# A first bias row picked earlier, late modulation steps behind the context's scalings, and the last context product behind the rows' sums

## Chip, cores and metric

The kernel runs on one core of one Trainium2 chip. The metric is the device time of one execution in microseconds, the median of several runs.

## What is computed

Two transformer blocks in sequence, all in float32. x is 256 rows by 1024.

```python
# block 1: attention (two kinds), then a mixture of 32 experts, 4 per row
x = x + gate1 * mixed
h2 = rms_norm(x, norm2_g) * (1 + scale2) + shift2
# per expert: act = (u + 1) * g * sigmoid(1.702 g), g, u clipped; y = act @ w_down + b_down
x = x + gate2 * moe_ffn(h2, ...)

# block 2: two layers on x and on a context xc of 256 rows
for l in range(2):
    mod, modc = silu(c) @ ada_w[l] + ada_b[l], silu(c_ctx) @ ada_w[l] + ada_b[l]
    h  = modulate(rms_norm(x,  mix_pre_g[l]), sh1,  sc1)
    hc = modulate(rms_norm(xc, mix_pre_g[l]), shc1, scc1)
    p = h @ w_in[l]                      # q, k, v, gated MLP, convolution, three gates
    attn = attention(q, [kc; k], [vc; v])  # the rows see the context's keys and values
    y = (ga * attn@w_a + gg * gmlp@w_g + gc * conv@w_c) @ w_out
    x = x + g1 * rms_norm(y)
    x = x + g2 * rms_norm(relu(modulate(rms_norm(x)) @ w1)**2 @ w2)
    if l == 0: the same mixer and MLP for xc, with its own modulation
```

The context's own mixer of layer 0 doesn't depend on x.

## The kernel before

**Weights.** All large weights come from one DRAM array, `stream`, in chunks of 1 MB. SyncE issues them in the order in which they are used into `ring`, a ring of six slots; a slot is filled again when TensorE has counted up `weights_used` for the chunk that was in it. Modulation weights of block 2 are loaded by GpSimd into other buffers.

**Experts.** The stage has 33 experts (e = 0 to 32; the last is a second pass of the expert with most rows). Each works on 64 gathered rows with 12 chunks: four for the gate product, four for the up product (both L862), four for the down product (L970). On TensorE an expert is: wait for the turned inputs (copied by ScalarE, L2495), bias products (L872, they wait for the bias row picked by VectorE: L1893 for expert 0, L1804 for the others), gate product, gather of rows in expert 0 (L879), up product, turning of the next inputs (L899), context work, transposes of the hidden rows (L962), context work, the wait for ScalarE's copy of them (L2514), down product. VectorE clips and multiplies (L1825 to L1845); ScalarE copies the outputs (L2522). The last expert differs: VectorE sums up all experts' rows and gates them (L1789, L1791), then multiplies the last down product by its gate (L1869); two scatters (L904) with a sum each (L1903) end the stage.

**The context's mixer in the experts' gaps.** The mixer of layer 0 for the context is cut into 50 heavy steps (a chunk each, 16 products over 256 columns, L771 or L775) and 41 light ones (transposes, scores, the convolution's mean `mu` and variance `var`). `_place()` (from L86) lays them into the experts: per expert two places for heavy steps, A ahead of the hidden rows' transposes and B behind them, and three for light ones, l1 (after A), l2 (after B) and l3 (after the down product). A heavy step is placed when those it depends on are two moments back and fewer heavy steps are placed than `quota` allows, which grows in a straight line over 65 slots. Experts 33 to 40 are places only; they stand behind the experts. The plan also sets the stream's order: the chunks of A and B come ahead of the expert's ninth chunk. Each engine has its own `context_at(e)` for the same plan. Step `("wo", 3)` is the last: behind it ScalarE sums the squares of both context row tiles (L2288) and VectorE scales and adds them to the context (L1640, L1642; marks `("L0", "x1", 2)` and `("L0", "x1", 3)`). Its buffer `yc` overlaps the first slots of `tmp`.

**Ahead of expert 0** VectorE makes the first selection (`choose(first, 0)`, L1548), four columns of tokens, `busiest()` (the most used expert; among it the reduction L1520 that makes the one-hot columns of experts 0 to 31 from the identity), takes sums of modulations (L1879), normalises the context's rows (L1543), and then copies the first column (L1893).

**Layer 0 of block 2** begins when x is complete: ScalarE's squares (L2288), VectorE's normalisation (L1543), transposes (L573), scalings (`modulated`, L1959), then the products of the convolution's gated pairs (L541 with `features`, eight pairs; ScalarE's sigmoids L2566, VectorE's products L1997). In it VectorE also does the modulation sums of later stages as single steps between its other work: the generators `middle_sums` and `gate_sums` (L1581, L1584 and two foldings). `gate_sums` has 72 steps over four loads; they are taken behind the eight conv products (`take_one("conv", f)`, L2163): 5 each, 18 more behind the fourth and 14 more behind the eighth. Then VectorE scales the context's rows for the MLP (`modulated((L, "h2", 0), ...)`), which TensorE transposes ahead of the output product (`mixed`, L1176); the residual (L1223, L2214, L2217) follows that product's first row tile. GpSimd adds the branches (L2729) and loads modulation weights (L2721) when the sums two loads back are done.

Of the kernel before, what the change touches and what calls it, by code (L numbers as in the profile page):

```python
# [78 lines left out]
def _place():  # L79
# [21 lines left out]
    for pos in range(first, (NBLK + 8) * len(PLACES)):  # L101
        e, w = divmod(pos, len(PLACES))
        w = PLACES[w]
        now = 10 * e + MOMENT[w]
        ready = lambda s: all(done.get(d, now) <= now - (14 if s == ("mu",) else 2) for d in after.get(s, []))
        if w in "AB":
            slots = 2 * (NBLK - START) - 1
            quota = -(-(2 * (e - START) + (w == "B")) * len(HEAVY) // slots)
            if heavy and ready(heavy[0]) and len(HEAVY) - len(heavy) < quota:
                place[e, w] = heavy.pop(0)  # L110
                done[place[e, w]] = now
        else:
            for s in light:
                if ready(s):
                    light.remove(s)
                    place[e, w] = s
                    done[s] = now
                    break
# [109 lines left out]
class Signals:  # L228
# [14 lines left out]
    def mark(self, name, *keys, inc=1):  # L243
        name = self.prefix + name
        self.count[name] = self.count.get(name, 0) + inc
        for key in keys:
            assert (self.prefix, key) not in self.marks, key
            self.marks[self.prefix, key] = (name, self.count[name], self.tag)
        return self.sem(name), inc
# [36 lines left out]
def build(nc, args, known, per):  # L286
    stream, mods_d, mods2_d, cols_d, rows_d, cst_d, x_d, ctx_d, ws_d, wr_d, bd_d, bgu_d, out_d = args
    with ExitStack() as ctx:
# [924 lines left out]
        def _(dve):  # L1213
# [296 lines left out]
            def busiest():  # L1510
# [6 lines left out]
                V.tensor_copy(stat("top"), idx[:, TT, 0:1]).then_inc(*mark("vector_steps"))  # L1517
                TS(stat("over1"), most[:, 0:1], float(2 * CAP), None, ALU.is_gt).then_inc(*mark("vector_steps"))
                TS(stat("over2"), most[:, 1:2], float(CAP), None, ALU.is_gt).then_inc(*mark("vector_steps"))
                V.tensor_reduce(onehot[:, 0:NE], ident.rearrange("p (r e) -> p e r", e=NE), AX, ALU.add).then_inc(*mark("vector_steps"))  # L1520
                dve.wait_ge(*last("vector_steps"))
                TT_(stat("over"), stat("over1"), stat("over2"), ALU.max).then_inc(*mark("vector_steps"))
                TS(onehot[:, NE:NBLK], con("index", 1), stat("top"), None, ALU.is_equal).then_inc(*mark("vector_steps"))
# [22 lines left out]
            def choose(tag, e):  # L1546
                for t in range(TT):
                    i = TS(sel[:, t, :], iot[:, 0:CAP], slot[:, bass.ds(e, 1), t], None, ALU.is_equal)  # L1548
                i.then_inc(*mark("selected", (tag, "sel")))
# [336 lines left out]

            first = ("first", "moe")
            choose(first, 0)
            for n in range(4):
                TS(stat("token", 4)[:, n:n + 1], con("lane", 1), float(P * n), None, ALU.add).then_inc(*mark("vector_steps"))  # L1890
            busiest_then(first)
            iotae_b = con("iotae", NE).unsqueeze(1).unsqueeze(1).to_broadcast([P, TT, TOPK, NE])
            V.tensor_copy(pickrow, onehot[:, 0:1].to_broadcast([P, CAP])).then_inc(*mark("row_picked", (first, "row")))  # L1893
            places()
            for e in range(NBLK):
                prev = ("moe", e - 1) if e else first
# [1 line left out]
            for t in range(TT):  # L1898
# [3 lines left out]
                    xs = x[:, t, 512 * h:512 * h + 512]  # L1902
                    i = TT_(xs, xs, ps[:, 6 + h, :], ALU.add)  # L1903
                i.then_inc(*mark("sums_updated", (tag, "y+", t)))
            for e in range(NBLK, NBLK + 8):
                for place in PLACES:
                    context_at(e)(place)
            dve.wait_ge(*at("flag"))
            over = nc.vector.value_load(flag[0:1, 0:1], min_val=0, max_val=1)
            with nc.vector.If(over > 0):  # L1910
# [54 lines left out]
            for l in range(LAYERS):  # L1965
# [5 lines left out]
                if l == 0:  # L1971
                    coefficients(0, (0,))
                    modulated((L, "h"), [(0, TT, 0)], 0)
                V.memset(glp[:, :, :, 0:PADT], 0.0).then_inc(*mark("vector_steps"))
                dve.wait_ge(*last("vector_steps"))
                V.memset(glp[:, :, :, SEQ + PADT:SEGW], 0.0).then_inc(*mark("vector_steps"))
# [223 lines left out]
                for f in range(KD):  # L2200
                    if f < 4:
                        dve.wait_ge(*at((L, "added", "attn", f + 4)))
                    take_one("conv", f)
                    for _ in range(5 + (18 if f == 3 else 14 if f == KD - 1 else 0)):
                        next(gates, 0)
                for _ in gates:
                    pass

                def residual(which, t, ready):

# [7 lines left out]
                    dve.wait_ge(*last("x_updated"))  # L2218
                if l == 0:
                    modulated((L, "h2", 0), [(TT, 2 * TT, 1)], 24)  # L2220
                for t in range(nt):
                    residual(0, t, "x1")
                    normalise(L, "n2", t, "xn2")
                    if l:
                        modulated((L, "h2", t), [(t, t + 1, 0)], 24)
# [47 lines left out]
        def _(act):  # L2273
# [257 lines left out]
            context_squares()  # L2531
            for e in range(NBLK):
                expert(("moe", e), e >= STORED, e < NE, (e,), context_at(e))
            for e in range(NBLK, NBLK + 8):
                for place in PLACES:
                    context_at(e)(place)
            act.wait_ge(*at("flag"))
            over = nc.scalar.value_load(flag[0:1, 0:1], min_val=0, max_val=1)
            with nc.scalar.If(over > 0):
# [10 lines left out]
            for l in range(LAYERS):  # L2550
# [7 lines left out]
                if l == 0:  # L2558
                    for t in range(TT):
                        sumsq((("L0", "n1"), t), rowsx[t:t + 1], junkb, [("x2", t)])  # L2560
                for k in range(KD):
                    kb = ((L, "cg"), 2 * k + 1)
                    act.wait_ge(*at(("full", kb)))
                    if k >= 4:
                        act.wait_ge(*at(("drained", ((L, "cg"), 2 * k - 8))))
                    A(tmp[:, k % 4, 0:N], ps[:, B(kb), 0:N], ACT.Sigmoid).then_inc(*mark("gates_ready", ("drained", kb)))  # L2566
# [394 lines left out]
```

## Time and profile before

| | us |
|---|---|
| median of 3 runs | 3087.0 (3080.79 to 3092.16) |
| the profiled execution | 3087.64 |
| its span | 3085.8 |
| TensorE busy | 2912.4 |
| VectorE busy | 1269.2 |
| ScalarE busy | 459.8 |
| GpSimd busy | 80.9 |

The span runs from the first to the last instruction. A busy TensorE is not one at its peak: matmuls are pipelined and their ends are modelled. The mean granted TensorE clock was 0.984 of full speed. The transfers moved 762.08 MB, 247 GB/s over the span; the experts' stage, from about 280 us to 1535, runs near 400 GB/s.

In the rows further down a window gives its length, the busy time (and count of instructions) of PE (TensorE's matmuls), PEld (its weight loads), DVE (VectorE), ACT (ScalarE) and POOL (GpSimd), the granted TensorE clock, the mean busy share of the DMA engines and what they moved. A row of the timeline gives start, duration, engine, line, operation, output and input and the count of instructions merged, and in brackets the idle time of that engine just before and who ended it.

### The profile page before, as it was taken

The numbers are of one execution on the slowest core, as the hardware profiler recorded it, in microseconds if no ns is written. First come the engines' busy times: TensorE is split into PE (matmuls) and PEld (weight loads), VectorE is DVE, ScalarE is ACT, GpSimd is POOL, SyncE is SP. The second block draws the span as 40 slices with busy tenths as digits, with TensorE's granted clock in tenths as the row PEclk, the third lists the DMA queues.
The fourth block names the chain that finished last, engine by engine and source line by source line (L and its number), as shares of the span: only waits on it lengthen the run. The fifth ranks groups of instructions, "written<-read, shape, count | busy, mean of one in ns | idle before, by whom it ended". The sixth has DMA issues, their size and how long they took to land.

```text
span 3085.8 us, 31210 instructions
## 1 busy us (share of the span) xinstructions
PE 2912.4 (94%) x12164; PEld 1724.0 (56%) x12164; DVE 1269.2 (41%) x3060; ACT 459.8 (15%) x921; POOL 80.9 (3%) x107
## 2 busy tenths in 40 slices
PE   5998999999999999998799999999999999999998
PEld 3464455555545444444387588544444677587764
DVE  6754112444441121111368856383582268731101
ACT  1212001222211110000202131110000111311100
POOL 0000000000000000001000001000000000000000
PEclk9988999999999999999999999999999999999999
DMA  8556999999999989999753324342441344124342
GB/s 330 223 225 268 405 387 394 389 399 395 394 399 387 398 359 402 392 406 401 321 196 144 137 76 177 115 176 97 163 164 55 109 149 149 57 109 164 111 163 95
DMA packets 110497, 762.08 MB, mean 247 GB/s; under 512 B 12976, under 2 KB 13360, under 8 KB 21776
## 3 DMA queue, kind: packets, MB, share of 16 engines
q1 hardware_dynamic: 95040, 699.44, 57.3%
q0 software_dynamic: 8240, 45.88, 4.0%
q10 hardware_dynamic: 7072, 14.76, 1.3%
q8 instruction: 99, 1.62, 0.2%
q14 instruction: 46, 0.38, 0.0%
HBM read 749.81 MB, written 10.22 MB: 246 GB/s over the span
## 4 chain that ended last, share of the span: by engine, by line
PE 82%; DMA 10%; DVE 6%; ACT 1%; issue 1%; DVEq 0%; SPq 0%; ACTq 0%
PE ps L541 26%; PE ps L553 17%; DMA ring<-stream 9%; PE ps L862 8%; PE ps L775 8%; PE ps L970 7%; PE ps L771 3%; PE ps L1176 2%; PE ps L1164 1%; PE ps L573 1%; PE ps L602 1%; PE ps L872 1%; PE ps L615 1%; DMA area<-modulation 1%; DVE area L1242 1%
## 5 line engine op out<-in xcount | busy, mean ns | idle before, releaser
L541 PE MATMUL ps<-area,ring 128*128 128x256 f32 (+1 forms) x3328 | 820.8, 409 | 0.3
L541 PEld LDWEIGHTS ps<-area,ring 128*128 128x128 f32 x3328 | 633.3, 191 | 183.8 <-issue 108.1
L553 PE MATMUL ps<-ring,area 128*128 128x512 f32 x1216 | 528.4, 596 | 4.0 <-DVE area L2263 4.0
L862 PE MATMUL ps<-ring,area 128*64 128x512 f32 x2112 | 479.7, 599 | 40.6 <-DMA ring<-stream 40.0
L553 PEld LDWEIGHTS ps<-ring,area 128*128 128x128 f32 x1216 | 232.0, 191 | 290.9 <-issue 285.3
L862 PEld LDWEIGHTS ps<-ring,area 128*64 128x64 f32 x2112 | 142.3, 137 | 376.1 <-issue 268.9
L775 PE MATMUL ps<-area,ring 128*128 128x256 f32 x1152 | 255.5, 380 | 0.0
L970 PE MATMUL ps<-ring,area 128*64 128x512 f32 x1056 | 237.1, 602 | 9.2 <-ACT area L2514 9.2
L775 PEld LDWEIGHTS ps<-area,ring 128*128 128x128 f32 x1152 | 216.0, 190 | 28.5
L2015 DVE SCALAR_TENSOR_TENSOR area<-area,cols 128x256 f32<-128x256 f32 x480 | 201.7, 483 | 1.1
L1584 DVE SCALAR_TENSOR_TENSOR cst<-area,cond,cst 128x256 f32<-128x256 f32 x448 | 183.0, 482 | 0.0
L970 PEld LDWEIGHTS ps<-ring,area 128*64 128x64 f32 x1056 | 73.6, 138 | 152.7 <-issue 141.7
L1840 DVE TENSOR_SCALAR area<-ps 128x512 f32<-128x512 f32 x33 | 22.8, 691 | 239.3 <-PE ps L862 239.3
L573 PE MATMUL ps<-cst,area 128*128 128x128 f32 x416 | 70.6, 311 | 40.7 <-DVE area L1959 17.5
L1825 DVE TENSOR_SCALAR area<-ps 128x512 f32<-128x512 f32 x33 | 22.8, 692 | 208.8 <-PE ps L862 208.8
L771 PE MATMUL ps<-ring,area 128*128 128x256 f32 x448 | 101.3, 385 | 3.6 <-ACT area L2506 2.3
L2248 DVE TENSOR_TENSOR area<-area 128x512 f32<-128x512 f32 (+1 forms) x64 | 34.7, 556 | 163.4 <-ACT area L2681 162.8
L1617 DVE SCALAR_TENSOR_TENSOR area<-area,cols 128x256 f32<-128x256 f32 x240 | 97.8, 477 | 0.1
L573 PEld LDWEIGHTS ps<-cst,area 128*128 128x128 f32 x416 | 55.0, 160 | 71.1 <-issue 41.8
L771 PEld LDWEIGHTS ps<-ring,area 128*128 128x128 f32 x448 | 85.2, 193 | 15.8 <-ACT area L2506 2.5
L1804 DVE COPY area<-area 128x64 f32<-128x64 f32 x32 | 6.2, 192 | 186.2 <-PE ps L872 186.2
L2681 ACT ACTIVATE area<-ps 128x512 f32<-128x512 f32 (+1 forms) x64 | 31.4, 491 | 294.3 <-PE ps L541 262.1
(342 smaller groups left out, 2043.6 us busy)
## 6 DMA issues: line engine op xcount, KB each, us to landing
ring<-stream SPq DMA_DIRECT2D x642, 1024.0 KB, 8.8
area<-shared_modulation POOLq DMA_DIRECT2D x32, 1024.0 KB, 5.1
area<-modulation SPq DMA_DIRECT2D x16, 1536.0 KB, 6.6
expert_rows<-area ACTq DMA_DIRECT2D x62, 128.0 KB, 7.2
x<-x_tiles ACTq DMA_DIRECT2D x1, 1024.0 KB, 12.9
area<-ctx_tiles ACTq DMA_DIRECT2D x1, 1024.0 KB, 4.9
input_rows<-area ACTq DMA_DIRECT2D x4, 256.0 KB, 2.0
out<-x SPq DMA_DIRECT2D x2, 512.0 KB, 2.6
```

What stands on the lines that cost most here:

```text
L541: i = mm(ps[:, b, 0:n], w[:, k % 4, j * P:(j + 1) * P], rhs(k), start=(k == 0), stop=(k == 4 * kgs - 1))
L553: i = mm(ps[:, b, :], lhs(k, t), w[:, k % 4, :], start=(k == 0), stop=(k == 4 * kgs - 1))
L573: i = nc.tensor.transpose(ps[:, b, j * P:(j + 1) * P], src(j), ident)
L771: ins = mm(ps[:, b, j * SEQ:(j + 1) * SEQ], src[:, k, j * P:(j + 1) * P], w[:, k, :], start=(k == 0), stop=(k == KD - 1))
L775: ins = mm(ps[:, b, j * SEQ:(j + 1) * SEQ], w[:, k, j * P:(j + 1) * P], src, start=(k == 0), stop=(k == KD - 1))
L862: i = mm(ps[half(h), bank, :], xT[:, k % 4, half(k // 4)], w[:, 2 * (k % 2) + h, :], start=False, stop=(k == KD - 1))
L970: i = mm(ps[half(h), APART if apart else DOWN, :], actT[:, k % 4, half(k // 4)], w[:, 2 * (k % 2) + h, :], start=(k == 0), stop=(k == KD - 1))
L1176: i = mm(ps[:, b, :], merged[:, k, t * P:(t + 1) * P], chunk(c)[:, k % 4, :], start=(k == 0), stop=(k == KD - 1))
L1584: i = STT(acc, w[:, k], c, acc, ALU.mult, ALU.add)
L1617: i = STT(cvc(k), src, w(k, tap), cvc(k), ALU.mult, ALU.add)
L2015: i = STT(dst, src, w(k, tap), dst, ALU.mult, ALU.add)
L2248: TT_(hid[:, j, 0:NF], tmp[:, j % 8, 0:NF], tmp[:, j % 8, 0:NF], ALU.mult).then_inc(*mark("hidden_ready", (L, "hid", hf, j)))
```

## The change

In `_place()` the quota grows over two slots more. The reduction leaves `busiest()`; it and the copy of the first bias row follow the first selection. The loops over the places of experts 33 to 40 move on VectorE behind layer 0's first scalings, and on ScalarE behind the squares of x, where a wait for the context's last addition is added ahead of the first sigmoid. TensorE's loop stays where it was, behind the last scatter. The last 19 of the `gate_sums` steps move from behind the eighth conv product to behind the scaling of the context's rows. The loader and the plan of the stream follow the placement.

```diff
@@ _place
-            quota = -(-(2 * (e - START) + (w == "B")) * len(HEAVY) // slots)
+            quota = -(-(2 * (e - START) + (w == "B")) * len(HEAVY) // (slots + 2))
@@ vector: busiest
-                V.tensor_reduce(onehot[:, 0:NE], ident.rearrange("p (r e) -> p e r", e=NE), AX, ALU.add).then_inc(*mark("vector_steps"))
@@ vector: ahead of the experts
             choose(first, 0)
+            V.tensor_reduce(onehot[:, 0:NE], ident.rearrange("p (r e) -> p e r", e=NE), AX, ALU.add).then_inc(*mark("vector_steps"))
+            dve.wait_ge(*last("vector_steps"))
+            V.tensor_copy(pickrow, onehot[:, 0:1].to_broadcast([P, CAP])).then_inc(*mark("row_picked", (first, "row")))
             for n in range(4):
                 TS(stat("token", 4)[:, n:n + 1], con("lane", 1), float(P * n), None, ALU.add).then_inc(*mark("vector_steps"))
             busiest_then(first)
             iotae_b = con("iotae", NE).unsqueeze(1).unsqueeze(1).to_broadcast([P, TT, TOPK, NE])
-            V.tensor_copy(pickrow, onehot[:, 0:1].to_broadcast([P, CAP])).then_inc(*mark("row_picked", (first, "row")))
             places()
@@ vector: behind the rows' last sums
-            for e in range(NBLK, NBLK + 8):
-                for place in PLACES:
-                    context_at(e)(place)
             dve.wait_ge(*at("flag"))
@@ vector: layer 0
                     coefficients(0, (0,))
                     modulated((L, "h"), [(0, TT, 0)], 0)
+                    for e in range(NBLK, NBLK + 8):
+                        for place in PLACES:
+                            context_at(e)(place)
@@ vector: conv branch
-                    for _ in range(5 + (18 if f == 3 else 14 if f == KD - 1 else 0)):
+                    for _ in range(0 if f == KD - 1 else 23 if f == 3 else 5):
                         next(gates, 0)
-                for _ in gates:
-                    pass
...
                 if l == 0:
                     modulated((L, "h2", 0), [(TT, 2 * TT, 1)], 24)
+                    for _ in gates:
+                        pass
@@ scalar: behind the experts
-            for e in range(NBLK, NBLK + 8):
-                for place in PLACES:
-                    context_at(e)(place)
             act.wait_ge(*at("flag"))
@@ scalar: layer 0
                     for t in range(TT):
                         sumsq((("L0", "n1"), t), rowsx[t:t + 1], junkb, [("x2", t)])
+                    for e in range(NBLK, NBLK + 8):
+                        for place in PLACES:
+                            context_at(e)(place)
+                    act.wait_ge(*at(("L0", "x1", 2 * TT - 1)))
```

## Rows read from the trace of the kernel before

**Rows 1.** Page, the chain that ended last, by engine.

```profile
PE 82%; DMA 10%; DVE 6%; ACT 1%; issue 1%; DVEq 0%; SPq 0%; ACTq 0%
```

**Rows 2.** Windows by expert, from one down product (L970) to the next.

```profile
333.22:373.78 40.56, 38.08 (x186) 19.89 (x188) 4.78 (x11) 2.81 (x5) 0.95 (x1) 1.00 1.00 413
...
608.48:642.78 34.30, 32.62 (x166) 15.61 (x168) 14.64 (x37) 7.56 (x12) 0.95 (x1) 1.00 0.98 399
...
832.22:860.07 27.85, 26.53 (x146) 11.08 (x148) 16.71 (x41) 2.42 (x4) 0.95 (x1) 1.00 1.00 400
...
860.07:903.33 43.26, 40.51 (x198) 21.83 (x200) 20.50 (x50) 6.69 (x12) 0.94 (x1) 1.00 0.96 396
...
1054.95:1101.21 46.26, 44.10 (x217) 26.16 (x216) 16.43 (x31) 10.85 (x16) 0.94 (x1) 1.00 0.85 335
...
1357.70:1397.49 39.79, 38.01 (x186) 20.06 (x188) 3.78 (x9) 2.91 (x5) 0.95 (x1) 1.00 0.98 408
...
1397.49:1430.31 32.82, 30.81 (x152) 13.95 (x153) 4.83 (x10) 2.91 (x5) 0.94 (x1) 1.00 0.98 389
```

**Rows 3.** Timeline around expert 0, several engines.

```profile
268.89 0.41 DVE L1548 TENSOR_SCALAR area<-cst,area 128x64 f32<-128x64 f32 x2
...
270.24 0.37 DVE L1520 TENSOR_REDUCE area<-cst 128x32 f32<-128x128 f32 x1
...
273.80 0.60 ACT L2495 ACTIVATE area<-ps 128x512 f32<-128x512 f32 x1 [1.77 <-PE ps L899]
...
279.61 0.19 DVE L1893 COPY area<-area 128x64 f32<-128x64 f32 x1
...
279.94 1.98 PE L872 MATMUL ps<-area 32*64 32x512 f32 x8 [6.18 <-DVE area L1893]
...
281.85 8.82 PE L862 MATMUL ps<-ring,area 128*64 128x512 f32 x32
...
292.22 7.03 PE L862 MATMUL ps<-ring,area 128*64 128x512 f32 x32
...
310.86 1.09 PE L872 MATMUL ps<-area 32*64 32x512 f32 x8
```

**Rows 4.** Window of two microseconds ahead of expert 0.

```profile
276.00:278.00 2.00, 0.00 (x0) 0.00 (x0) 0.74 (x2) 1.99 (x3) 0.00 (x0) 0.50 0.00 0
```

**Rows 5.** Timeline of the last two experts and layer 0's begin.

```profile
1467.34 7.17 PE L771 MATMUL ps<-ring,area 128*128 128x256 f32 x32
...
1506.84 8.86 PE L771 MATMUL ps<-ring,area 128*128 128x256 f32 x32 [2.26 <-ACT area L2506]
...
1516.37 1.06 ACT L2288 ACTIVATE area<-area 128x1024 f32<-128x1024 f32 x1
...
1520.64 0.59 ACT L2514 ACTIVATE area<-ps 128x512 f32<-128x512 f32 x1
...
1521.29 8.62 PE L970 MATMUL ps<-ring,area 128*64 128x512 f32 x32 [4.93 <-ACT area L2514]
...
1530.53 0.69 DVE L1869 TENSOR_TENSOR area<-ps,area 128x512 f32<-128x512 f32 x1
...
1533.89 1.13 PE L904 MATMUL ps<-area 64*128 64x512 f32 x4 [1.48 <-DVE x L1903]
...
1542.33 3.65 PE L573 MATMUL ps<-cst,area 128*128 128x128 f32 x16 [7.31 <-DVE area L1543]
...
1554.14 0.38 ACT L2566 ACTIVATE area<-ps 128x256 f32<-128x256 f32 x1 [11.64 <-PE ps L541]
```

**Rows 6.** Timeline in layer 0 between the conv branch and the residual.

```profile
1924.50 0.42 DVE L2163 TENSOR_TENSOR area<-ps,area 128x256 f32<-128x256 f32 x1
...
1934.42 2.04 PE L573 MATMUL ps<-cst,area 128*128 128x128 f32 x8 [9.14 <-DVE area L1959]
...
1936.26 28.22 PE L1176 MATMUL ps<-ring,area 128*128 128x512 f32 x64
...
1952.59 0.15 DVE L1223 TENSOR_SCALAR stats<-stats 128x1 f32<-128x1 f32 x1 [15.06 <-ACT area L2288]
```

## The prediction

> **What bounds the kernel now.** I read the chain of waits first [rows 1]: matmuls hold 82% of it, transfers 10%, VectorE 6%. So time is saved only where TensorE stands idle, runs at the lower of its clock levels, or takes turns with the weight stream. The windows by expert [rows 2] show the last: each window runs from one expert's down product to the next one's. With two heavy context steps it takes some 40 us, and TensorE is busy for 38 of them. With one it takes 33 to 34; TensorE is busy for 31 to 33 of them and the transfer share is 0.98. So TensorE sets an expert with two steps, the stream one with fewer. The timeline ahead of the first expert [rows 3] shows TensorE idle for 6.18 us until VectorE has copied the first bias row. The one around the last expert [rows 5] shows it waiting 4.93 us for ScalarE's copy and 7.31 us for the rows' scaling. The one in layer 0's mixer [rows 6] shows 9.14 us of idle time ahead of the transposes of the second row set.
>
> **First bias row, and the reduction that feeds it.** The copy (0.19 us) starts at 279.61 because the normalisation of the context's rows stands ahead of it [rows 3]. It needs only a reduction of a constant (0.37 us). Both now follow the first selection, which ends at 269.30; they are through by about 269.9. TensorE's next condition is ScalarE's copy of the turned inputs, which ends at 274.40 [rows 3]. So the biases start at about 274.45, 5.5 us earlier. Behind the old place of the copy stand VectorE's row numbers and the selection for the next gather. They keep their times, some 2 us after 279.61, and TensorE wants the selection only after the gate product, at 274.45 + 1.09 + 7.03 = 282.6: just in time. The idle time also costs clock: the granted clock is 0.50, the 1.2 GHz level, at 276 to 278 [rows 4]. The biases take 1.98 us there and 1.09 at the upper level, the first gate product 8.82 and 7.03 [rows 3]: 2.7 us more. The stream cannot hold this back: it moves 0 GB/s at 276 to 278 [rows 4], since the ring's six chunks are full and the first is freed by the gate product; it restarts earlier by the same 8.2 us. I take **-8.2**; if the clock falls all the same, -5.5; nothing if another wait stood at 279.9, for which no row speaks.
>
> **Planner's quota.** I worked out the placement from the rule as the code has it. Before: experts 0 and 1 none, then two steps in 20 experts up to 31, one in 9, none in expert 15, one in 32. After: two in 18, one in 12, expert 15 gets one, one in 32, and the last step (wo, 3) in slot 33, behind the experts. The 17 undisturbed windows with two steps (first and last of them shown) average 39.71 us, the 9 with one (first and last shown) 33.86. The window without a step takes 27.85, but its successor 43.26, so with the carry it is worth 31.4 [rows 2]. The change up to expert 31: 2 x 39.71 + 31.4 against 3 x 33.86, that is -9.2 us. Of this 5.85 is the step that leaves, the rest comes from evening out. Bounds: if bytes alone counted, one chunk of 1.05 MB at 400 GB/s [rows 2], -2.6; on the other side -9.2.
>
> Two places within it differ. The context's variance step moves from ahead of ScalarE's copy for the down product to behind it, with a heavy step of TensorE over the mean step's squares. The window that holds it now has 46.26 - 44.10 = 2.2 us of idle TensorE [rows 2]; I take **-2.2**, bounds 0 and -3.8 (with the slower down product behind such a wait, 8.62 against 7.03 [rows 5]). In expert 9 the step (qkv, 5) now stands alone in the first slot, with its square, root and VectorE's sum ahead of that same copy and no second heavy step over it. The nearest row is the 4.93 us wait of the last expert [rows 5]; most of it falls into time in which such an expert waits for the stream, so +1.0, bounds 0 and +4.9. Together **-10.4**.
>
> A page of the Trainium skill speaks against this term. "DMA: Bandwidth & Descriptors", Where 436 GB/s comes from, says that the HBM side binds transfers into SBUF at about 358 GB/s per core. The windows but the disturbed one show 389 to 413 GB/s [rows 2], so the trace doesn't agree. By the rule the 13 chunks of a window with one step (13.6 MB) would need 38 us, every expert would be set by bytes, and the term would be one chunk, an estimated -2.9; the sum would be that of the first rival.
>
> **The last expert and what follows.** Now (wo, 3) runs in the last expert's first slot: 8.86 us of TensorE, then on ScalarE a copy, two passes of squares (from 1516.37) and a root with an answer from VectorE, and only then the copy for the down product at 1520.64, so the down product starts at 1521.29 and takes 8.62 at a fallen clock. VectorE does four context operations and four of the totals, and its product of the last rows starts at 1530.53 [rows 5]. After: (wo, 2) stands in the second slot, behind the transposes of the hidden rows and beside ScalarE's copy. 1506.84 + about 1.0 for two groups of transposes + 8.86 + 7.03 without the idle time = 1523.7. VectorE's totals need only the gate row of 1506.8 and end by 1512. The product of the rows comes 6.5 us earlier, and the two scatters with it.
>
> (wo, 3) then falls into TensorE's 7.31 us between the last scatter and the transposes [rows 5]. At the upper level it takes 7.17, and the first transpose, which takes its bank, also waits for ScalarE's 0.6 us copy: +0.5. In return TensorE keeps its clock: the first sigmoid now stands at 1554.14, 8.2 us after the transposes, where a pair of features is 16 products like a context step's, 7.17: -1.0. Queued behind the moved VectorE part (about 5 us of four additions and scalings) are the padding and the first gated product; ScalarE's added wait stands ahead of its first sigmoid. Both are due about 8 us after the transposes begin to be scaled, as now, and TensorE has four banks, nearly 14 us, before it needs one back. I cost this at nothing; without that cover it would be up to 11 us. Together **-7.0**; bounds -2 and -8.5.
>
> **Late modulation steps.** The 19 steps behind the last conv product ran from 1924.92 (end of that product [rows 6]) until the scaling on which the transposes wait for 9.14 us. Moved behind the scaling they free it at 1924.9; the transposes resume about 0.6 us later, at 1925.5 instead of 1934.42. **-8.9**. The output product then starts at about 1927.3 instead of 1936.26. The steps, 9 us on VectorE, now run to about 1937.7; what follows them is the residual, due 16.3 us after the output product's start (1952.59 - 1936.26), so at 1943.6: 6 us to spare. GpSimd's next modulation load follows them by some 4 us, and nobody reads it before the next stage. Bounds -6 and -9.7 (the clock no longer falls in the gap).
>
> **The sum.** -8.2 - 10.4 - 7.0 - 8.9 = -34.5 us. From the profiled execution's 3087.64 us (span 3085.8 and 1.8 around it) this gives **3053 us**; the median of the runs is 3087.0, so it needs no shift.
>
> **Rivals.**
> *The stream sets the experts.* Bytes don't change; if TensorE's share of an expert is only borrowed from the ring's store, the quota gives one chunk's time. For it: a transfer share of 0.96 and more in all windows shown but the disturbed one. Against it: 5.85 us per step instead of 2.6. 3087.6 - 8.2 - 2.6 - 7.0 - 8.9 = 3061.
> *The last context step becomes the wait.* ScalarE stands at the added wait while TensorE fills its banks: 11 us back (about 4 of squares and root, 5 of VectorE, the rest between them). For it: the root needs VectorE, which is at the scalings. Against: four banks. 3064.
> *Slower: context steps in the second slot hold ScalarE and VectorE when the next expert needs them.* Twelve steps move from first to second slot in their expert. If each cost what the variance step does, 2.2 of idle time and 1.6 of clock, that is 46 us, and the sum 3099. It decides from the tenth such stall. Against it: the copy that the down product needs now stands ahead of them, and the down product (7 us) and the next gate product (7 us) cover them.
> *The gain is given back.* The earlier start is lost before the end, because something not in these rows has its own time: 3083. Nothing in the layers is timed otherwise than by TensorE.
>
> **Chances.** Forecast 0.65, stream 0.20, last step 0.08, slower 0.04, given back 0.03. Range: from all terms at their better ends with the runs' scatter, 3043, to the first two rivals with a term short, 3069. A measurement of this kernel tells about 0.5%, 15 us, from no change. All but the last two cases lie beyond it on the fast side: faster 0.92, same 0.05, slower 0.03.
>
> **What would show it.** The copy of the first bias row at about 270, the first gate product in 7.0 us and a clock of 1.00 ahead of it. Windows of 34 and 39.7 us, 12 and 18 of them. No idle time of TensorE ahead of the last down product, (wo, 3) behind the last scatter. The output product directly behind the second row set's transposes. It would be wrong if windows with one step took 36 us or more, if the first sigmoid came more than 9 us after the transposes, or if the residual waited for the modulation steps.

## The result and the profile after

| | before | after |
|---|---|---|
| median | 3088.58 us (4 runs) | 3054.99 us (4 runs) |
| range | 3080.79 to 3092.16 | 3053.54 to 3056.72 |
| span of the profiled execution | 3085.8 | 3052.6 |
| TensorE busy | 2912.4 | 2903.9 |
| mean granted clock | 0.984 | 0.990 |

The ratio is 0.9898, with a 95% interval of 0.9886 to 0.9910: 31.5 us faster by the ratio (the two medians differ by 33.6, the profiled spans by 33.2). In a later series the same kernel had 0.9896 (0.9878 to 0.9915). Bytes are unchanged (762.08 MB), and so is the chain by engine but for a point [rows 1]:

```profile
PE 83%; DMA 9%; DVE 5%; ACT 1%; issue 1%; DVEq 0%; SPq 0%; ACTq 0%
```

**Ahead of expert 0.** The timeline of the changed kernel, several engines, against [rows 3]:

```profile
269.21 0.42 DVE L1547 TENSOR_SCALAR area<-cst,area 128x64 f32<-128x64 f32 x2
...
269.94 0.20 DVE L1890 COPY area<-area 128x64 f32<-128x64 f32 x1
...
274.12 0.60 ACT L2496 ACTIVATE area<-ps 128x512 f32<-128x512 f32 x1 [1.77 <-PE ps L899]
...
274.82 1.40 PE L872 MATMUL ps<-area 32*64 32x512 f32 x8 [0.73 <-issue]
...
276.14 8.42 PE L862 MATMUL ps<-ring,area 128*64 128x512 f32 x32
```

and the window against [rows 4]:

```profile
276.00:278.00 2.00, 2.00 (x10) 0.63 (x8) 0.42 (x2) 1.97 (x3) 0.00 (x0) 0.50 0.00 0
```

The copy is at 269.94 and the biases follow ScalarE's copy of the turned inputs, as forecast. But the clock is at its lower level, 1.2 GHz, in this window although TensorE is busy through all of it, and the gate product takes 8.42 us, not 7.03. Expert 0's down product starts at 297.22 (before 303.33): 28.0 us after the start of the selection at 269.21, against 34.4 before. That is 6.4 us.

**The windows by expert**, from down product to down product, against [rows 2]:

```profile
565.24:597.99 32.75, 32.18 (x166) 15.75 (x168) 15.95 (x38) 7.78 (x15) 0.94 (x1) 1.00 0.99 406
597.99:635.23 37.24, 32.75 (x167) 15.59 (x168) 15.24 (x37) 8.72 (x14) 0.95 (x1) 1.00 1.01 419
...
821.69:856.51 34.82, 33.46 (x179) 17.15 (x180) 17.47 (x42) 7.71 (x14) 0.94 (x1) 1.00 1.01 410
856.51:896.81 40.30, 39.74 (x202) 22.30 (x204) 22.23 (x54) 6.30 (x11) 0.94 (x1) 1.00 0.96 390
...
1042.67:1090.00 47.33, 44.84 (x218) 26.07 (x220) 7.33 (x13) 7.22 (x11) 0.94 (x1) 1.00 0.89 362
1090.00:1122.41 32.41, 30.52 (x154) 14.07 (x156) 13.37 (x26) 6.53 (x10) 0.94 (x1) 1.00 0.93 375
```

They are experts 8, 9, 15, 16, 21 and 22. From expert 0's down product to expert 31's it is 1164.24 us, before 1171.19: -6.95, where -10.4 was forecast. The one-step windows but expert 9's average 33.5 us, the two-step ones but experts 21 and 31 39.9. Expert 9's takes 37.24.

**The last expert and layer 0's begin**, against [rows 5]:

```profile
1495.19 8.18 PE L771 MATMUL ps<-ring,area 128*128 128x256 f32 x32
...
1503.31 7.09 PE L970 MATMUL ps<-ring,area 128*64 128x512 f32 x32
...
1510.51 0.69 DVE L1868 TENSOR_TENSOR area<-ps,area 128x512 f32<-128x512 f32 x1 [11.67 <-PE ps L970]
...
1514.92 7.17 PE L771 MATMUL ps<-ring,area 128*128 128x256 f32 x32
...
1522.79 2.94 PE L573 MATMUL ps<-cst,area 128*128 128x128 f32 x16 [0.69 <-ACT area L2433]
...
1534.01 0.38 ACT L2568 ACTIVATE area<-ps 128x256 f32<-128x256 f32 x1
1534.53 0.42 DVE L1998 TENSOR_TENSOR area<-ps,area 128x256 f32<-128x256 f32 x1 [1.25 <-ACT area L2568]
```

(wo, 2) runs straight into the down product, (wo, 3) lies behind the last scatter, and the transposes wait 0.69 us instead of 7.31. From the first bound, expert 31's down product, to the last product (L1868) it is 49.1 us, before 56.1: -7.0. From there to the transposes 12.28 against 11.80: +0.5. From the transposes to the second sigmoid 16.79 against 18.71: -1.9.

**The second row set's transposes**, against [rows 6]:

```profile
1903.45 1.80 PE L573 MATMUL ps<-cst,area 128*128 128x128 f32 x8 [0.15 <-DVE area L1957]
...
1920.90 0.15 DVE L1223 TENSOR_SCALAR stats<-stats 128x1 f32<-128x1 f32 x1 [5.48 <-ACT area L2289]
```

The output product starts at 1905.09, 2.82 us after the first set's transposes (1902.27), before 12.02: -9.2. It and its surroundings last 28.62 us against 29.24: -0.6. The residual finds VectorE idle for 5.48 us, so the moved steps are hidden.

The sum: +0.3 (the selection came later) - 6.4 - 6.95 - 7.0 + 0.5 - 1.9 - 9.2 - 0.6 = -31.3 of the -33.2 between the two spans. 0.5 more lies in layer 0 between, and 1.4 in the 1100 us behind, spread over many stages; I did not follow it.

### The profile page after: what moved, and what is told of

The parts are those of the page before. It is cut to its first block, busy times and chain, and to the rows that moved or that the text cites. A ratio compares the mean times of both kernels' runs of the same rounds, so it can differ in the third digit from the quotient of the medians.

```text
span 3052.6 us, 31208 instructions
## 1 busy us (share of the span) xinstructions
PE 2903.9 (95%) x12164; PEld 1719.6 (56%) x12164; DVE 1269.7 (42%) x3060; ACT 457.1 (15%) x919; POOL 80.7 (3%) x107
## 2 busy tenths in 40 slices
DMA packets 110497, 762.08 MB, mean 250 GB/s; under 512 B 12976, under 2 KB 13360, under 8 KB 21776
## 4 chain that ended last, share of the span: by engine, by line
PE 83%; DMA 9%; DVE 5%; ACT 1%; issue 1%; DVEq 0%; SPq 0%; ACTq 0%
PE ps L541 27%; PE ps L553 17%; DMA ring<-stream 9%; PE ps L862 8%; PE ps L775 8%; PE ps L970 7%; PE ps L771 3%; PE ps L1176 2%; PE ps L1164 1%; PE ps L573 1%; PE ps L602 1%; PE ps L872 1%; PE ps L615 1%; DMA area<-modulation 1%; DVE area L1242 1%
## 5 line engine op out<-in xcount | busy, mean ns | idle before, releaser
L862 PE MATMUL ps<-ring,area 128*64 128x512 f32 x2112 | 478.7, 599 | 38.1 <-DMA ring<-stream 37.5
L970 PE MATMUL ps<-ring,area 128*64 128x512 f32 x1056 | 235.4, 598 | 0.0
L970 PEld LDWEIGHTS ps<-ring,area 128*64 128x64 f32 x1056 | 73.2, 137 | 142.4 <-issue 142.0
L573 PEld LDWEIGHTS ps<-cst,area 128*128 128x128 f32 x416 | 53.3, 156 | 56.8 <-issue 34.4
```

Source lines behind the costliest of these rows:

```text
L573: i = nc.tensor.transpose(ps[:, b, j * P:(j + 1) * P], src(j), ident)
L862: i = mm(ps[half(h), bank, :], xT[:, k % 4, half(k // 4)], w[:, 2 * (k % 2) + h, :], start=False, stop=(k == KD - 1))
L970: i = mm(ps[half(h), APART if apart else DOWN, :], actT[:, k % 4, half(k // 4)], w[:, 2 * (k % 2) + h, :], start=(k == 0), stop=(k == KD - 1))
```

## Experiments

Each is given by its edit against the kernel before or the changed one. Kernels of a series share their runs of the kernel before; its medians were 3087.0, 3085.6, 3087.9 and 3091.4 us, so the ratios are compared, not the times. Of e8_clock there is one run, of e10_half there are two.

### One part alone

**e1_row**, on the kernel before:

```diff
             choose(first, 0)
+            V.tensor_reduce(onehot[:, 0:NE], ident...)
+            V.tensor_copy(pickrow, onehot[:, 0:1]...)      # both deleted at their old places
```

> Only the first bias row and its reduction are moved. Theory, after the trace of the changed kernel (biases 5.1 us earlier, gate product still 8.42 us): the term stands alone and is worth 6 us, ratio 0.9980. Rival 1, the prediction's own term: 8.2 us, ratio 0.9973. Rival 2, the start is lost again within the experts because the stream has its own time: under 2 us, ratio 0.9994 or more.

Measured: 0.9980 (0.9971 to 0.9989), 6.2 us. In its profiled execution the clock did not fall; TensorE's timeline:

```profile
277.51 1.09 PE L872 MATMUL ps<-area 32*64 32x512 f32 x8 [0.73 <-issue]
278.53 7.09 PE L862 MATMUL ps<-ring,area 128*64 128x512 f32 x32
```

The down product comes 26.3 us after the selection, against 33.7 to 34.4 in the four profiles with the copy at its old place: there the forecast's term of 8.2 is nearly reached. In six profiles of kernels that share the changed kernel's order here (it, its repetition, and e5, e6, e7 and e9 below) the gate product took 8.36 to 8.57 us and the distance was 27.9 to 28.0; in a seventh, of e10 below, 9.26 and 29.4.

**e2_late**, on the kernel before:

```diff
-                    for _ in range(5 + (18 if f == 3 else 14 if f == KD - 1 else 0)):
+                    for _ in range(0 if f == KD - 1 else 23 if f == 3 else 5):
...
                     modulated((L, "h2", 0), [(TT, 2 * TT, 1)], 24)
+                    for _ in gates:
+                        pass
```

> Only the late modulation steps are moved. Theory: the idle time ahead of the second row set's transposes goes from 9.14 us to under 0.3, the output product takes 27.5 us instead of 28.2 and nothing behind it is late: 9.8 us, ratio 0.9968. The prediction had 8.9, ratio 0.9971. Rival: the steps delay the residual or the next load and part comes back: 6 us or less, ratio 0.9981 or more.

Measured: 0.9973 (0.9963 to 0.9983), 8.3 us. It agrees with 8.9 as with 9.8, but the interval reaches down to 5.2 us, so the runs alone don't exclude the rival's 6. The trace does, as far as one goes:

```profile
1926.68 27.63 PE L1176 MATMUL ps<-ring,area 128*128 128x512 f32 x64
...
1942.49 0.15 DVE L1223 TENSOR_SCALAR stats<-stats 128x1 f32<-128x1 f32 x1 [5.47 <-ACT area L2288]
```

The output product starts 2.82 us after the first set's transposes, the MLP's first product follows 28.62 us later, both as in the changed kernel, and the residual finds VectorE idle.

**e3_plan**, the kernel before with the quota and the moved loops:

```diff
-            quota = -(-(...) * len(HEAVY) // slots)
+            quota = -(-(...) * len(HEAVY) // (slots + 2))     # and both loops moved, as in the change
```

> Quota and moved loops, without the other two parts. Theory: 7.0 us up to the last expert's down product, 7.0 in the last expert, 1.4 behind it: 15.4 us and, with what the two traces leave unassigned, up to 17; ratio 0.9950. The prediction had 17.4 us (0.9944). Rival, the stream sets the experts: 2.6 + 7.0 = 9.6 us, ratio 0.9969. If the parts only add up together (a faster part uncovers another), this one and the two single parts sum to less than the 33.6 us of the whole.

Measured: 0.9960 (0.9946 to 0.9974), 12.3 us. The rival's 0.9969 lies in the interval too. The three sum to 26.9 us with some 6 us of uncertainty; 31.5 for the whole is inside it. The parts add up as far as can be told.

**e4_quota**, the quota alone, both loops at their old place.

> The quota alone: the loops over the places behind the experts stay in VectorE's and ScalarE's old place, ahead of the rows' squares. The last context product is then on TensorE behind the last scatter, and ScalarE's copy, squares and root and VectorE's additions stand ahead of the squares of x. Theory: 11 us of the gain come back (7.2 of product, 4 of ScalarE and VectorE), so 4 us faster than before, ratio 0.9986, and TensorE idle for some 18 us ahead of the transposes. Rival, the loops' place is worth nothing because the product lies in a gap anyway: as with the loops moved, 0.995.

Measured: 1.0009 (1.0000 to 1.0018): not 4 us faster but 3 slower. The timeline at layer 0's begin, three engines:

```profile
1524.50 7.17 PE L771 MATMUL ps<-ring,area 128*128 128x256 f32 x32
...
1540.46 1.22 DVE L1642 TENSOR_TENSOR area<-area 128x1024 f32<-128x1024 f32 x1
...
1542.17 1.06 ACT L2288 ACTIVATE area<-x 128x1024 f32<-128x1024 f32 x1 [4.42 <-DVE stats L1933]
...
1547.74 3.65 PE L573 MATMUL ps<-cst,area 128*128 128x128 f32 x16 [16.06 <-DVE area L1543]
```

From the last product to the transposes it is 27.65 us instead of 12.28, so the place of the loops is worth 15.4 us, more than quota and last expert together. I had expected 11, the product and ScalarE's part, and left out VectorE's additions, which end only at 1541.7 with the squares of x behind them. The quota by itself gains nothing. The moved loops by themselves hold no step, since with the old quota (wo, 3) lies in the last expert; only together do the two gain.

**e5_noquota**, the changed kernel with the old quota (`// slots`).

> The changed kernel with the old quota: 50 steps in the experts, nothing in the moved loops. Theory, the quota is worth what the trace of the changed kernel shows (7.0 us up to the last expert's down product, 7.0 in the last expert, 0.5 lost and 1.9 won behind it): 15.4 us slower than the changed kernel, ratio to before 0.9948. If the run with quota and loops alone tells the size (12.3 us), ratio 0.9938. Rival, the stream sets the experts: 9 us slower than the changed kernel, ratio 0.9927. The idle time ahead of the first transposes should be 7.3 us again and the last down product should wait some 5 us for ScalarE.

Measured: 0.9944 (0.9930 to 0.9958), 14 us slower than the changed kernel, between the two sizes that the theory gave; the stream's 0.9927 is just outside. Both waits came back:

```profile
1514.39 10.09 PE L970 MATMUL ps<-ring,area 128*64 128x512 f32 x32 [4.93 <-ACT area L2515]
...
1536.39 3.65 PE L573 MATMUL ps<-cst,area 128*128 128x128 f32 x16 [7.30 <-DVE area L1542]
```

### How much cover there is

**e6_cover**, on the changed kernel:

```diff
                         r = rstd_of(("C", "y"), TT, D)
+                        for _ in range(8):
+                            TT_(yc[:, 0, :], yc[:, 0, :], yc[:, 0, :], ALU.max)...
```

> The changed kernel, with eight more VectorE operations of about 1.23 us on the first context row tile between the root and the scalings of the last context step (they leave its values as they are): the added wait ends some 9.9 us later. Theory, four banks cover: the first gated product stood at 1534.5 and TensorE needs the first bank back two pairs (13.8 us) after its first product at 1525.6, so 4.9 us are spare and 5 of the 9.9 us show: idle TensorE of 5 us in the features' products, ratio 0.9914. Rival 1, no cover, the wait was already on the path: 9.9 us, ratio 0.993. Rival 2, nothing of it is on the path: 0.9898.

Measured: 0.9925 (0.9912 to 0.9939), 8 us slower. TensorE, timeline:

```profile
1526.25 13.98 PE L541 MATMUL ps<-area,ring 128*128 128x256 f32 x64
...
1544.56 30.70 PE L541 MATMUL ps<-area,ring 128*128 128x256 f32 x129 [4.33 <-DVE area L2001]
```

TensorE ran for 13.98 us, two pairs, into its four banks and then waited 4.33 us. That is the forecast's cover with its length. But the idle time had a second price: the granted clock was 0.63 from 1542 to 1546, the end of the wait included, and 0.52 from 1546 to 1550, and from the first product of the features to the transposes behind the conv branch it was 384.2 us against 376.7 in the changed kernel, 7.5 for an idle time of 4.3. The interval includes rival 1's 0.993; the trace rules it out.

**e7_spare**, on the changed kernel:

```diff
                     for _ in gates:
                         pass
+                    for _ in range(10):
+                        TT_(x[:, 0, :], x[:, 0, :], x[:, 0, :], ALU.max)...
```

> The changed kernel, with ten more VectorE operations of about 1.23 us on the first row tile (values as they are) behind the moved modulation steps: 12.3 us more ahead of the residual. Theory: the residual had 5.5 us to spare (its idle time in the changed kernel), so it comes 6.8 us late; what follows it on TensorE is the transposes of the rows for the MLP behind the output product, so up to 6.8 us show if nothing else lies over them, ratio up to 0.992. Rival 1, the spare is larger because TensorE is still in the second row tile of the output product: 0, ratio 0.9898. Rival 2, the steps already held the residual: all 12.3 us, 0.9938.

Measured: 0.9912 (0.9897 to 0.9928), 4 us slower. The residual came 7.2 us late by the trace, as expected. Of these, TensorE's wait ahead of the MLP's first product (L1164) shows 2.95 us instead of 1.00, and the product took 15.59 us instead of 14.05 at a granted clock of 0.66 from 1939 to 1943: 3.5 us. So beyond VectorE's 5.5 us there are about 5 more in which only VectorE is late, under the second row tile of the output product.

### What sets an expert

**e10_half**, on the changed kernel:

```diff
                 for j in range(2):
-                    for k in range(KD):
+                    for k in range(0, KD, 2):          # in context_heavy of TensorE; stop= moved to match
```

> The changed kernel with half of the products left out of every heavy context step (16 of 32, so 3.55 us of 7.1 us of TensorE; the context's values are therefore not computed); every byte is still loaded. Theory: an expert with two steps is set by TensorE (39.9 us), one with one step by the stream (33.5 us for 13 chunks, 2.58 us each). With half the products two steps take 14 chunks, 36.1 us, and one step still 33.5: 18 x 3.8 = 68 us less, the transfer share near 1.00 in all windows; about 2985 us, ratio 0.967. Rival 1, the stream sets every window already: under 10 us less, ratio 0.987. Rival 2, TensorE sets every window: 30 x 1.6 x 3.55 = 170 us less, ratio 0.935.

Measured: 0.9680 (0.9649 to 0.9710), 0.967 expected. Windows of experts 7 (two steps), 8 (one), 11 (two) and 12 (one):

```profile
510.85:546.92 36.07, 32.12 (x157) 14.08 (x156) 14.48 (x36) 6.87 (x11) 0.94 (x1) 1.00 1.01 420
546.92:582.05 35.13, 30.29 (x150) 12.19 (x149) 16.94 (x42) 7.53 (x15) 0.95 (x1) 1.00 1.01 421
...
652.21:688.25 36.04, 33.62 (x165) 15.72 (x164) 17.07 (x40) 9.11 (x16) 0.95 (x1) 1.00 1.01 420
688.25:721.96 33.71, 30.32 (x149) 12.68 (x148) 15.76 (x39) 7.99 (x14) 0.94 (x1) 1.00 1.01 422
```

Look at the last two columns: with half of the context steps' products gone the stream runs at 420 GB/s in these windows (415 to 423 in 29 of the 32 windows from expert 1 on; less in 21, 22 and 32), and 55 chunks (experts 5 to 8) take 144.1 us, 2.62 each. At that pace an expert with two steps costs some 36 us and one with one step 34. So in the changed kernel a two-step expert (39.9) is set by TensorE and a one-step expert (33.5) by the stream, and a step more or less is worth about 6 us, not one chunk.

**e9_turn**, on the changed kernel, for the wait in expert 9:

```diff
 PLACE = _place()
+PLACE[9, "l2"], PLACE[9, "l3"] = PLACE[9, "l3"], PLACE[9, "l2"]
```

> The changed kernel with two light steps of expert 9 in each other's place: (score, 1) ahead of the down product, (turn, 5) behind it. In the changed kernel (turn, 5) waits 2.66 us for VectorE ahead of the down product, since (qkv, 5) stands alone in the first slot and no heavy step covers its norm. Theory: the window of expert 9 goes from 37.2 to 34.6 us and most of it stays: 2 to 2.7 us, ratio 0.989. Rival, the stream takes it: the window's transfer share is 1.01, so the product waits for the same chunk two experts on and nothing is won, 0.9898.

TensorE's waits in the changed kernel from 290 to 1540 (engine, line, for whom, us, times, longest):

```profile
PE ps L862 <- DMA ring<-stream: 37.5, 65, 1.6
PE ps L962 <- DVE area L1844: 12.6, 10, 1.4
PE ps L797 <- DVE area L1678: 2.7, 1, 2.7
```

and in the kernel before:

```profile
PE ps L862 <- DMA ring<-stream: 40.0, 68, 1.7
PE ps L970 <- ACT area L2514: 9.2, 5, 4.9
PE ps L962 <- DVE area L1845: 7.8, 7, 1.4
```

Measured: 0.9885 (0.9870 to 0.9901), not told apart from the changed kernel. The wait of 2.66 us is replaced by one of 1.18 for ScalarE, the windows of experts 9 and 10 are

```profile
597.25:633.55 36.30, 33.17 (x167) 15.89 (x168) 14.27 (x34) 9.41 (x15) 0.95 (x1) 1.00 1.01 420
633.55:673.68 40.13, 39.36 (x198) 21.68 (x200) 17.94 (x44) 8.13 (x15) 0.95 (x1) 1.00 0.93 376
```

0.9 shorter and 0.6 longer than in the changed kernel's profile (37.24 and 39.52): 0.3 us for both, which looks like the rival. But the sum of these two windows varies by itself: in seven profiles with the changed plan (the changed kernel, e3, e4, e6, e7, e8 and e12) it is 76.8 to 79.9 us with a mean of 78.2, and the changed kernel's own is the least of them. Here it is 76.4, and 76.1 in e11_more below. So the theory's 2 us and the rival's nothing both stay possible, in the trace as in the runs.

**e11_more**, on the changed kernel, three edits:

```diff
+PLACE[9, "B"] = PLACE.pop((9, "A"))
+PLACE[9, "l2"], PLACE[9, "l3"] = PLACE[9, "l3"], PLACE[9, "l2"]
+PLACE[22, "l2"] = PLACE.pop((21, "l2"))
...
-            for n in range(PAIRG + 2, PAIRG + PAIRL):
-                fold_pair(n)
+            fold_pair(PAIRG + 2)
             turn_rows(first)
+            fold_pair(PAIRG + 3)
```

> The changed kernel with three more edits of the order: (qkv, 5) alone in the second slot of expert 9 with (turn, 5) behind the down product; the variance step one expert later, in expert 22, which has one heavy step and waits for the stream; expert 0's inputs turned between the two foldings ahead of it. Theory: 3 us (expert 9's window from 37.2 to some 34), 1.5 us (expert 21's 47.3 us lose 3.6 of TensorE work, expert 22's 32.4 take it partly into waits for the stream), 0.6 us: 5 us faster than the changed kernel, ratio to before 0.988. Rival, stalls taken away only let the stream fall behind, and the waits for it take all of it back: ratio as of the changed kernel.

**e12_again**, the changed kernel unaltered, in the same series.

> The changed kernel once more, on the same chip as the one above: 0.9898 as the first time if the other kernels' differences of 3 to 6 us are to be read at their face value; its interval says how far they can be.

Measured: 0.9879 (0.9860 to 0.9897) for e11_more and 0.9896 (0.9878 to 0.9915) for e12_again. That e11_more beats the changed kernel isn't shown. The windows of its experts 9, 21 and 22:

```profile
594.24:629.90 35.66, 33.20 (x166) 15.75 (x168) 14.55 (x36) 7.66 (x13) 0.94 (x1) 1.00 1.01 420
...
1042.81:1086.00 43.19, 41.16 (x203) 23.09 (x204) 7.76 (x15) 5.34 (x9) 0.94 (x1) 1.00 0.91 377
1086.00:1123.01 37.01, 34.41 (x170) 16.96 (x172) 4.41 (x8) 4.30 (x6) 0.94 (x1) 1.00 0.98 396
```

Expert 21 gave 4.1 us and expert 22 took 4.6: the moved step's 3.6 us of TensorE work only changed places. TensorE's wait for VectorE in (turn, 5) is gone from the stage, and so is the one for ScalarE that e9_turn had in its place. The waits of the gate and up products for the stream were 43.6 us, against 37.5 in the changed kernel and 34.3 to 39.7 in the seven profiles with its plan. From expert 0's to expert 31's down product it took 1170.6 us, no less than in those (1161.6 to 1169.9). The third edit shows ahead of expert 0: the clock stayed, and its down product came 25.8 us after the selection instead of 28.0.

```profile
273.30 7.09 PE L865 MATMUL ps<-ring,area 128*64 128x512 f32 x32
```

### The clock ahead of expert 0

**e8_clock**, on the changed kernel:

```diff
+            for d in range(8):
+                mm(ps[half(d % 2), GATE, :], ident[:, 0:64], xn1[:, d % 2, 0:512], start=True, stop=True)
             turn_rows(first)
+            for d in range(4):
+                mm(...)                                     # the same
```

> The changed kernel with twelve extra products of 128x512 into a bank that is overwritten later: eight ahead of the turning of expert 0's inputs (1.8 us), four between it and the biases. Theory, the clock falls because TensorE has idle time and only narrow products (128x2, 128x128) there: with wide products it stays at 1.00, the biases take 1.09 us and the gate product 7.03 instead of 1.40 and 8.42; the down product of expert 0 comes 1.8 - 1.7 = 0.1 us later than in the changed kernel, counted from the first selection (27.9 us there). Rival, the fall has nothing to do with what TensorE does in these few us: the gate product still takes 8.4 us and the down product comes 29.7 us after the selection.

TensorE's timeline:

```profile
277.10 3.65 PE L992 MATMUL ps<-area,cst 128*64 128x512 f32 x16
...
281.27 1.94 PE L995 MATMUL ps<-area,cst 128*64 128x512 f32 x8
283.14 1.09 PE L872 MATMUL ps<-area 32*64 32x512 f32 x8
284.15 7.09 PE L862 MATMUL ps<-ring,area 128*64 128x512 f32 x32
```

The clock stayed, as the theory has it. The size was off: a product counts as two instructions of 0.23 us each, so the twelve take 5.6 us, and the down product came 31.0 us after the selection, 3.1 later than in the changed kernel. One profile doesn't prove the cause, since e1_row kept its clock without them, and e11_more kept it with a folding moved behind the turning and no more idle time than 0.35 us ahead of the biases. As a gain the twelve products are useless: they cost more than the clock gives back.

## Why the prediction was right, step by step

3053 was forecast, 3055 came. Part of that is luck: by the two traces two terms were too large by 5 us, two too small by 2, and 2 lie where nothing was forecast.

| step | forecast | the two traces | by runs |
|---|---|---|---|
| first bias row | -8.2 | -6.4 | -6.2 (-9.0 to -3.4) |
| quota, up to expert 31 | -10.4 | -7.0 | |
| last expert, (wo, 3), clock | -7.0 | -8.4 | |
| these two | -17.4 | -15.4 | -12.3 (-16.7 to -8.0) alone; -14 by taking the quota back |
| late modulation steps | -8.9 | -9.8 | -8.3 (-11.4 to -5.2) |

**First bias row.** The 5.5 us of idle time were right (the biases came 5.4 us earlier, counted from the selection). The 2.7 us of clock were the mis-sized term: 1.0 came back, since the clock fell with TensorE idle for only 0.73 us, behind two foldings of narrow products and four transposes. The fallback named there, -5.5, was nearer (0.9 us off, and the value taken 1.8). Whether it falls isn't settled by the instructions alone: e1_row had the same ones here and kept 1.00. The Trainium skill's "TensorE: Matmul & The Clock Gate", What's actually happening, says that how many products run at the lower clock at a kernel's start differs between runs of one and the same kernel. The two profiles of the changed kernel don't show that (8.42 and 8.44 us for the gate product); the eight of kernels that are alike here do differ, in the middle of a kernel (7.09 once, 8.36 to 8.57 six times, 9.26 once). Why the clock fell in seven of the eight stays open.

**Quota.** The count of windows was right (18, 12, none without a step), and so was their price. Experts 8, 12, 14, 18 and 20 went from two steps to one and lost 32.4 us, 6.5 each; 11, 13 and 19 went the other way, +17.7; 15 and 16 together +4.0: -10.7, where the working had -9.2. Three things ate the rest, by these two profiles. Expert 9 took 2.9 us more, not 1.0. I had taken ScalarE's copy for the wait; it was the light step (turn, 5), which on TensorE stands ahead of the down product and needs VectorE's norm. I had counted moved heavy steps and not the light step that follows one. Experts 21 and 22 gave 1.7 us, not 2.2. There the wait for ScalarE of 2.17 us went, and the product behind it took 7.09 us instead of 8.74, as in the forecast's bound of 3.8; but the two experts' waits for the stream rose from 1.5 to 2.8. And the sixteen windows of experts 1 to 7, 10, 17 and 23 to 29, whose count of steps did not change, grew by 2.8 us together (30 and 31 gave 0.3). One thing in them is new: where the only step stands in the second slot, the hidden rows' transposes have no cover and wait for VectorE, 10 times and 12.6 us instead of 7 times and 7.8. What share of the 2.8 this is, I can't say: from expert 0's to expert 31's down product four profiles with the old placement took 1171.2 to 1173.5 us and seven with the new one 1161.6 to 1169.9, so a difference of 2 us in one of them is no finding. The means differ by 6.9. Expert 9's longer window is a finding: 36.6 to 37.7 us in the seven, 33.8 to 34.7 in the four.

What expert 9's wait costs the kernel isn't shown. With it removed, e9_turn and e11_more were 1.7 and 2.1 us below the mean of the seven in experts 9 and 10 together, within 0.7 us of the least of them, and neither kernel is told apart from the changed one. That the ring fills while TensorE waits, so that the next experts wait less for the stream and a stall costs less than its length, fits the longer waits for the stream in experts 21 and 22 and in e11_more; it is argued, not shown.

**The stream as a rival.** It had 0.20 and its time was 3061. e10_half settles the mechanism. By the rule of the Trainium skill's "DMA: Bandwidth & Descriptors", Where 436 GB/s comes from, quoted in the forecast, the stream could not pass 358 GB/s; here it held 420 to 422. The Trainium skill's "Perfetto Trace Analysis", Roofline, says that a core whose neighbour is idle can draw more than that share, up to about 435 GB/s of its DMA engines; this trace agrees with that page.

**Last expert.** -7.0 for 6.5, and +0.5 as forecast for (wo, 3) and its copy. The clock kept was worth 1.9, not 1.0. The rival "the last context step becomes the wait" was wrong for the reason that the forecast gave: the first gated product stood 5 us ahead of TensorE's need, and in e6_cover TensorE stopped where its four banks were full. e4_quota shows what the moved loops protect from: 15.4 us.

**Late modulation steps.** -9.8 for -8.9: the value taken left out that the clock no longer falls, which was in the bound (-9.7). The interval of the runs (-11.4 to -5.2) doesn't tell the two apart. The spare was 5.5 us where 6 was forecast.

**Slower rival.** It needed steps in the second slot to hold the down product (by the placement 13 moved there within their expert, not 12). In the changed kernel no down product waits for ScalarE for more than 0.2 us; five did before, for 9.2 us. What these steps cost is the missing cover of the first slot.

## What to carry over

Count a moved step by everything that stands in its old and new neighbourhood: the light step behind it that needs its result, and the transposes that it used to cover. Where two resources take turns (here TensorE in experts with two steps, the stream in those with one), level the load first; removing a single stall of 1 to 3 us gave nothing here that four or five runs could tell from noise. Before you read a window's change from two profiles, look how far it varies between profiles of the same plan (here up to 3 us for two experts). And two edits can be worth nothing or less each and 12 us together: try a move of work and a move of its waits as one.

## What I had not expected of the hardware

- TensorE's clock stood at 0.50 with TensorE busy for 2.00 of 2.00 us in the window at 276 to 278, behind 0.73 us of idle time, and was back at 1.00 by 280. A single wait of 4.33 us (e6_cover) was followed by granted clocks of 0.63 and 0.52 in two windows of 4 us, so it cost 7.5 us in all; the 4.93 us wait in e5_noquota made the down product behind it 10.09 us long instead of 7.02, 8.62 in the kernel before with the same wait.
- Executions differ by up to 5.8 us before the experts begin: the first selection stood between 267.2 and 273.0 us in fourteen profiles of kernels that are alike up to it, and at 269.21 and 267.39 in two of one kernel.
